# Opening, neighbourhood diagonals and feed forward of a two-block transformer kernel: transfers reordered, six feed-forward stages in one

## The reference

```python
def first_block(x, c, ctx, c_ctx, ...):
    for l in range(2):
        shift, scale, gate = split(silu(c) @ w_mod[l] + b_mod[l], 3)      # the same for c_ctx
        h = rms_norm(x, norm_gain[l]) * (1 + scale) + shift               # hc from ctx likewise
        aq, ak, av, ag, bz, bg, nq, nk, nv, ng = split(h @ w_in[l])
        ...          # global attention, pooling, neighbourhood attention
        # the latter adds bias = rpb[:, drow, dcol], a table of relative positions
        x = x + gate * (y @ w_out[l])
    return x

def second_block(x, p, ...):
    ...              # forgetting attention and a recurrent scan
    h2 = rmsnorm(x, g_ffn)
    u = causal_dwconv(h2 @ w_up, conv_w, conv_b)          # D_FF = 2816: 2 x 22 tiles of 128
    x = x + (gelu(u[..., :D_FF]) * u[..., D_FF:]) @ w_down
    x = x + sigmoid(rmsnorm(x, g_ple) @ w_ple_gate) * (p @ w_ple_up)
    return x
```

## Time and profile before

| | us |
|---|---|
| median of 3 runs | 4183.56 |
| lowest and highest run | 4174.37, 4185.14 |
| the profiled execution | 4179.65 |
| its span, first to last instruction | 4177.9 |
| PE matmuls busy | 3622.6 (87% of the span) |
| DVE, POOL, ACT busy | 1949.7, 1606.7, 1147.7 |
| mean granted TensorE clock | 0.926 of full speed |

### The profile page before, as it was taken

The page is one execution under the profiler, slowest core; times in us unless marked ns, Lnnn a source line. Parts: engine busy times, 40 slices in busy tenths (PEclk is TensorE's granted clock), DMA queues, the critical chain, the costliest instruction groups (busy, mean ns, idle before and its releaser), DMA issues. The chain is left out here.

```text
span 4177.9 us, 59647 instructions
## 1 busy us (share of the span) xinstructions
PE 3622.6 (87%) x24988; PEld 2712.7 (65%) x24988; DVE 1949.7 (47%) x1943; ACT 1147.7 (27%) x1585; POOL 1606.7 (38%) x881
## 2 busy tenths in 40 slices
PE   4999699879899798888999977858798989989878
PEld 3788333668677334676777767734477777877767
DVE  4342566552542665533577023354543642633524
ACT  2223344330213343412344112225301320100122
POOL 0332356542343465434357333313333422423233
PEclk9999799989899799998999988868898999999989
DMA  4111200044112100122212210010041111111111
GB/s 164 36 39 66 62 1 1 14 157 148 54 36 72 19 1 14 55 108 78 81 48 77 84 42 4 4 70 1 21 160 41 45 40 45 46 45 41 39 44 68
DMA packets 93715, 226.52 MB, mean 54 GB/s; under 512 B 28320, under 2 KB 37920, under 8 KB 92464
## 3 DMA queue, kind: packets, MB, share of 16 engines
q1 hardware_dynamic: 85616, 193.86, 14.0%
q10 hardware_dynamic: 7872, 29.36, 2.0%
HBM read 184.36 MB, written 38.83 MB: 53 GB/s over the span
## 5 line engine op out<-in xcount | busy, mean ns | idle before, releaser
L265 PE MATMUL acc<-h_hi,weights_hi 128*128 128x512 f32 (+1 forms) x1152 | 452.3, 393 | 85.0 <-DVE h_lo L1879 39.7
L252 POOL TENSOR_TENSOR weights_hi<-weights,ones 128x1024 fp32r<-128x1024 f32 (+3 forms) x100 | 176.4, 1764 | 775.8 <-PE acc L267 775.8
L266 PE MATMUL acc<-h_lo,weights_hi 128*128 128x512 f32 (+1 forms) x1152 | 449.3, 390 | 0.0
L267 PE MATMUL acc<-h_hi,weights_lo 128*128 128x512 f32 (+1 forms) x1152 | 448.6, 389 | 0.0
L1637 PE MATMUL acc<-h_hi,weights_hi 128*128 128x512 f32 (+1 forms) x928 | 366.1, 395 | 32.3 <-DVE h_lo L1791 26.4
L1638 PE MATMUL acc<-h_lo,weights_hi 128*128 128x512 f32 (+1 forms) x928 | 340.3, 367 | 0.0
L1639 PE MATMUL acc<-h_hi,weights_lo 128*128 128x512 f32 (+1 forms) x928 | 340.3, 367 | 0.0
L957 DVE TENSOR_REDUCE part_max<-aux 128x2 f32<-128x856 f32 (+5 forms) x234 | 237.8, 1016 | 213.9 <-PE aux L823 147.6
L265 PEld LDWEIGHTS acc<-h_hi,weights_hi 128*128 128x128 f32 x1152 | 222.1, 193 | 133.2 <-issue 63.5
L2249 PE MATMUL acc<-h_hi,weights_hi 128*128 128x512 f32 x672 | 274.3, 408 | 24.8 <-DVE h_lo L2527 14.8
L1673 POOL TENSOR_TENSOR weights_hi<-weights,ones 128x1024 fp32r<-128x1024 f32 x44 | 85.7, 1947 | 498.3 <-PE acc L1639 389.2
(11 more groups left out here) (412 smaller groups left out, 7604.1 us busy)
## 6 DMA issues: line engine op xcount, KB each, us to landing
weights<-in_w_in SPq DMA_DIRECT2D x44, 512.0 KB, 3.5
weights<-in_w_up SPq DMA_DIRECT2D x41, 512.0 KB, 3.5
arena<-in_w_mod SPq DMA_DIRECT2D x6, 2048.0 KB, 9.8
weights<-in_w_out SPq DMA_DIRECT2D x21, 512.0 KB, 4.9
weights<-in_w_mod ACTq DMA_DIRECT2D x4, 2048.0 KB, 19.5
mixer_gates<-arena SPq DMA_DIRECT2D x32, 256.0 KB, 2.0
x_between<-arena ACTq DMA_DIRECT2D x16, 512.0 KB, 3.1
weights<-in_w_gates SPq DMA_DIRECT2D x16, 512.0 KB, 3.6
```

What stands on the lines that cost most here:

```text
L265: nc.tensor.matmul(out, w.hi[:, b, k, :], hi[:, kr, cols], start=(k == 0), stop=False)
L266: nc.tensor.matmul(out, w.hi[:, b, k, :], lo[:, kr, cols], start=False, stop=False)
L267: return nc.tensor.matmul(out, w.lo[:, b, k, :], hi[:, kr, cols], start=False, stop=(k == nk - 1))
```

## The change

- Opening: SP's queue takes the small loads, x tiles 0, 2, 4, 6, then w_mod pieces 0 and 2 and the first two tiles of w_in; ACT's queue takes ctx, x tiles 1, 3, 5, 7 and w_mod pieces 1 and 3. The spreading of rstd with its three copies and POOL's parting of the first two weight tiles move from `project` into `opening` for layer 0; the buffers for them are made before it. `project` skips them there.
- Diagonals: SP issues the lower half of each head, then the two gate pieces; ACT issues the upper half of each head, one ahead of each of its four key copies.
- Feed forward: one stage, `feed_forward`, with a list of jobs of known order. Parts are 7, 7 and 8 tiles. Of a part's ups the next part's first one is done ahead of the part's eight downs, except in the last part. Every engine's program is straight code over the jobs. The first down of a part takes its last k after all others in both chunks. The conv, gelu and gating are as before; the squares at the end use the buffers of the conv.

```diff
+        def diagonals(h):
+            return bass.AP(rpb.tensor, (l * NA_HEADS + h) * 15 * RPB_ROW, [[1, GRID_W], [RPB_ROW, 15], [1, GRID_W]])
...
                 for h in range(NA_HEADS):
                     sp.wait_ge(cleared, h + 1)
-                    for a in range(2):
-                        first = (l * NA_HEADS + h) * 15 * RPB_ROW
-                        src = bass.AP(rpb.tensor, first, [[1, GRID_W], [RPB_ROW, 15], [1, GRID_W]])
-                        sp.dma_start(diag[a * 64:a * 64 + 64, h, a:a + 15, :], src).then_inc(placed[h], 16)
-                    if h < 2 and gates:
-                        gates.fetch(sp, h)
+                    sp.dma_start(diag[0:64, h, 0:15, :], diagonals(h)).then_inc(placed[h], 16)
+                for i in range(2 if gates else 0):
+                    gates.fetch(sp, i)
...
                     for half in range(2):
+                        h = 2 * i + half
+                        act.wait_ge(cleared, h + 1)
+                        act.dma_start(diag[64:P, h, 1:16, :], diagonals(h)).then_inc(placed[h], 16)
                         nc.scalar.copy(k_twice[half * HD:(half + 1) * HD, i, :], k[i * HD:(i + 1) * HD]).then_inc(rounded, 1)
...
-                sp.dma_start(x[:, :, SEQ:TOK], I["ctx"]).then_inc(x_loaded, 16)
-                for k in range(KD):
+                for k in range(0, KD, 2):
                     sp.dma_start(x[:, k, 0:SEQ], I["x"][:, k]).then_inc(tile_loaded[k], 16)
+                for i in (0, 2):
+                    m.fetch(sp, i)
+                for j in range(2):
+                    sp.dma_start(raw[:, j], I["w_in"][0, j]).then_inc(w_loaded, 16)
 
             @block.scalar
             def _(act):
-                for i in range(4):
+                act.dma_start(x[:, :, SEQ:TOK], I["ctx"]).then_inc(x_loaded, 16)
+                for k in range(1, KD, 2):
+                    act.dma_start(x[:, k, 0:SEQ], I["x"][:, k]).then_inc(tile_loaded[k], 16)
+                for i in (1, 3):
...
+                for c, (c0, cw) in enumerate(BOTH):
+                    act.wait_ge(spread, c + 1)
+                    nc.scalar.copy(rstd_all[:, c0:c0 + cw], pg.aux[:, c % 2, 0:cw]).then_inc(kept, 1)
                 for i in range(4):
                     m.keep(act, i)
+                act.wait_ge(kept, 3)
+
+            @block.gpsimd
+            def _(pool):
+                pool.wait_ge(w_loaded, 32)
+                for j in range(2):
+                    nc.gpsimd.tensor_tensor(w_hi[:, j], raw[:, j], ones, ALU.mult).then_inc(w_rounded, 1)
+                    pool.wait_ge(w_rounded, j + 1)
+                    nc.gpsimd.tensor_tensor(w_lo[:, j], raw[:, j], full(w_hi[:, j]), ALU.subtract).then_inc(w_parted, 1)
+                pool.wait_ge(w_parted, 2)
...
+                pe.wait_ge(inverted, 1)
+                for c, (c0, cw) in enumerate(BOTH):
+                    if c == 2:
+                        pe.wait_ge(kept, 1)
+                    for t in range(cw // P):
+                        mm = nc.tensor.matmul(pg.aux[:, c % 2, t * P:(t + 1) * P], pg.rstd[:, c0 // P + t:c0 // P + t + 1].to_broadcast([P, P]),
+                                              cn["ident"][:], start=True, stop=True)
+                    mm.then_inc(spread, 1)
...
-                fetch(0)
-                fetch(1)
+                if not opened:
+                    fetch(0)
+                    fetch(1)
...
+                if opened:
+                    pool.sem_inc(parted, 2)
                 for kind, i in order:
-                    if kind == "split":
+                    if kind == "split" and i >= done_before:
                         b = i % 2
-                        pool.wait_ge(loaded[b], 16 * (i // 2 + 1))
+                        pool.wait_ge(loaded[b], 16 * ((i - done_before) // 2 + 1))
...
-                    for c, (c0, cw) in enumerate(BOTH):
+                    for c, (c0, cw) in enumerate(() if opened else BOTH):
...
+                weights = pg.sbuf(feats, "weights", [P, 2, KD, P]), *pg.pair(feats, "weights", [P, 2, KD, P])
+                if l == 0:
+                    opening(pg, cn, x, spare[-1], mods[0], given, cond, weights)
                 h = pg.pair(feats, "h", [P, KD, TOK])
-                project(pg, cn, l, x, h, mix, na, pool_z, spare, mods[l], *gains, gates_dram)
+                project(pg, cn, l, x, h, mix, na, pool_z, spare, mods[l], *gains, gates_dram, weights, l == 0)
...
+def feed_forward(pg, cn, x, h, conv, conv_b, g, maker_in):
...
+    parts = [(0, 7), (7, 7), (14, 8)]
+    jobs = []
+    for p0, n in parts:
+        jobs += [("up", i, b) for i in range(p0, p0 + n) for b in range(2) if ("up", i, b) not in jobs]
+        if p0 + n < FF_TILES:
+            jobs.append(("up", p0 + n, 0))
+        jobs += [("down", p0, t) for t in range(KD)]
+    part_of = dict(parts)
+    slot = {p0 + i: i for p0, n in parts for i in range(n)}
+    downs = [job for job in jobs if job[0] == "down"]
+    ups = lambda job: 2 * job[1] + job[2]
+    tail = parts[-1][0]
+
+    def weights(j):
+        kind, i, t = jobs[j]
+        if kind == "up":
+            return weight_tiles(w_up)(i + t * FF_TILES)
+        return w_down[t:t + 1, :, i:i + part_of[i], :].rearrange("t p k n -> p (t k) n")
+
+    def depth(j):
+        return KD if jobs[j][0] == "up" else part_of[jobs[j][1]]
...
+        total, ring = raw[:, 0, 2:], [u[:, 0], u[:, 1]]
...
+                for j in range(2, len(jobs)):
+                    sp.wait_ge(w.parted, j + 1)
+                    sp.dma_start(w.raw[:, j % 2, 0:depth(j)], weights(j)).then_inc(w.loaded[j % 2], 16)
...
+                for j in range(2, len(jobs)):
+                    kind, i, t = jobs[j]
+                    pe.wait_ge(w.parted, j + 3)
+                    if jobs[j - 2][0] == "up":
+                        pe.wait_ge(raw_ready, ups(jobs[j - 2]) + 1)
+                    else:
+                        pe.wait_ge(x_added, downs.index(jobs[j - 2]) + 1)
+                    rhs, nk = h if kind == "up" else g, depth(j)
+                    if kind == "down" and t == 0:
+                        pe.wait_ge(g_parted, i + nk - 1)
+                        for c0, cols in MAIN:
+                            for k in range(nk - 1):
+                                product(j, c0, cols, k, *rhs)
+                        pe.wait_ge(g_parted, i + nk)
+                        for c0, cols in MAIN:
+                            mm = product(j, c0, cols, nk - 1, *rhs)
+                    else:
+                        for c0, cols in MAIN:
+                            for k in range(nk):
+                                mm = product(j, c0, cols, k, *rhs)
+                    mm.then_inc(acc_ready, 1)
...
+                for j in range(2, len(jobs)):
+                    b, nk = j % 2, depth(j)
+                    pool.wait_ge(w.loaded[b], 16 * (j // 2) + 16)
+                    pool.wait_ge(acc_ready, j - 1)
...
+                for j, (kind, i, t) in enumerate(jobs):
+                    if kind == "up":
+                        act.wait_ge(acc_ready, j + 1)
+                        if i >= 1:
+                            act.wait_ge(raw_used, 2 * (i - 1) + t + 1)
+                        nc.scalar.copy(raw[:, t, 2:], pg.acc[:, j % 2, 0:SEQ]).then_inc(raw_ready, 1)
...
+                    elif i == tail:
+                        act.wait_ge(x_added, downs.index((kind, i, t)) + 1)
+                        if t >= 3:
+                            act.wait_ge(sq_added, t - 2)
+                        nc.scalar.activation(ring[t % 2] if t else total, x[:, t, 0:SEQ], ACT.Square).then_inc(sq_ready, 1)
...
+                        if t == 0 and i >= 1:
+                            dve.wait_ge(g_parted, i)
...
+                        if i == tail and t == 0:
+                            dve.wait_ge(g_parted, FF_TILES)
+                        dve.wait_ge(acc_ready, j + 1)
+                        tile = x[:, t, 0:SEQ]
+                        stt(tile, pg.acc[:, j % 2, 0:SEQ], 1.0, tile, ALU.mult, ALU.add).then_inc(x_added, 1)
+                        if i == tail and t >= 2:
+                            add_squares(t - 1)
...
-        for t0 in range(0, FF_TILES, FF_PART):
-            n = min(FF_PART, FF_TILES - t0)
-            norm = lambda u, rstd_all: Norm(pg, cn, xT, h, gain("g_ffn_2"), u, rstd_all)
-            feed_forward_up(pg, h, conv, cols["conv_b_2"], t0, n, g, norm if t0 == 0 else None)
-            w_down = lambda t: I["w_down_2"][bass.ds(t, 1), :, t0:t0 + n, :].rearrange("t p k n -> p (t k) n")
-            last = t0 + n == FF_TILES
-            with ExitStack() as own:
-                squares = pg.sbuf(own, "squares", [P, 3, SEQ])
-                gemm_residual(pg, cn, w_down, KD, g, xT, [(0, SEQ, None)], n, squares=[squares[:, b] for b in range(3)] if last else None)
-            pg.end_section()
+        norm = lambda u, rstd_all: Norm(pg, cn, xT, h, gain("g_ffn_2"), u, rstd_all)
```

(67 more changed lines are left out.)

81 lines of the change are left out of this document (34 added, 47 removed).

## The result

| | before | after |
|---|---|---|
| median of 4 runs each | 4184.35 us | 4085.94 us |
| lowest and highest | 4174.37, 4186.34 | 4083.74, 4088.41 |
| profiled execution, its span | 4179.65, 4177.9 | 4087.94, 4085.9 |
| mean granted clock | 0.926 | 0.936 |

The account below looks back on a forecast made before the run. TensorE bounds the kernel wherever weights stream, so only stretches where it stands can be won. Opening -20.5, diagonals -1.9, feed forward -62.9 give -85.3 from 4179.65; with 3.9 for the median, 4098 us, range 4083 to 4124.

Parts of the forecast that it names:

- Opening, -20.5: Opening: with x and ctx first and early w_in, the first product starts at 59.1 instead of 79.6, 20.5 us less.
- the two that are left then end by 50: Opening: w_mod's last two pieces land about 43, so the remaining two of four products with additions end by 50 us.
- The opening now waits for that: Opening: POOL's parting of both w_in tiles, ending at 53.3 us, was to be what ends the block.
- Diagonals of layer 1, +4.4: Second layer's diagonals: four issues on ACT's queue delay ACT and the stage by 4.4 us, between 2.8 and 6.
- 0.95 + 4 x 0.86: Second layer's diagonals: ACT's delay as one POOL clear of 0.95 us plus four issues of 0.86, together 4.4 us.
- Diagonals of layer 0, -6.3: First layer's diagonals: leading w_mod, they let the stage end near 448.5 instead of 454.76; -6.3 us, between 0 and -8.
- Feed forward, -62.9: Feed forward: five joins go, 64.6 us, less a new wait of 1.7; -62.9 us, between -64.6 and -52.
- The matmul term: Feed forward: 3072 matmuls from job 2 on at 0.2265 us each, at the upper clock level, take 695.9 us.
- ACT held by its queue: Rival, opening: ACT's issues hold it until about 27 us, taking 6.4 us off the gain, 4105 us; chance 0.08.
- The clock sinking in a long stretch: Rival, feed forward: 544 us beyond the longest shown stretch granted 0.95, 27 us lost, 4125 us; chance 0.05.
- Straight code that starves PE: Rival, feed forward: matmuls slow without loops; gain gone at 0.2543 us each, 4201 us at 0.26; chance 0.02.
- It does not do what it says: Rival, feed forward: PE still stands where ups and downs meet, three joins at 12.9 us, 4137 us; chance 0.04.

Follow-up runs that it names:

- weights_late: Changed kernel with the first two tiles of w_in again loaded and parted in the projection, the new transfer order kept; 4094.84 us.
- old_order: Changed kernel with the opening's transfers in the order of before, w_in behind x, the rest kept; 4111.83 us.
- diag_sp: Changed kernel with all eight diagonal transfers on SP's queue, still ahead of the gate pieces, none on ACT's; 4076.77 us.
- diag_only: Kernel before with only the diagonals' part of the change; 4171.40 us, ratio to before 0.9987.
- The two repeats: Changed kernel run again unaltered, twice, beside other versions; 4092.10 and 4091.08 us, ratios to before 0.9805 and 0.9797.
- late_join: Changed kernel where SP loads the first up tile's weights behind parts one and two only after the part's last down tile is added; 4113.63 us.

## Why the prediction was right, and where it was not

- *Opening, -20.5.* -21.0, and most steps came as forecast: w_in was seen at 43.66 (44.5 expected), POOL ended at 52.76 (53.3), DVE started at 53.59 (53.9), the first product came at 58.60 (59.1). One step was wrong and stayed hidden: "the two that are left then end by 50". PE began the first of the four products only behind the spreading, at 42.03, and even without POOL the last addition ends at 52.6 (weights_late, 52.47 + 0.17); here it ended at 53.06. So "The opening now waits for that", said of POOL's parting, holds by less than half a microsecond; had POOL been done at 50, the block would still have ended near 53. That this error cost nothing is luck. The gain of 7 because POOL no longer stands beside DVE is borne out by weights_late (8.6), and old_order shows the chain behind the squares setting the end.
- *Diagonals of layer 1, +4.4.* Right in sign and mechanism (diag_sp gives it back), wrong in size: +2.4. The failed term is "0.95 + 4 x 0.86": it put all four issues between ACT's copies, but an issue runs on the sequencer beside the copy before it. Only the wait for the clear, the first issue and 0.79 us of queue stand on the path, 0.95 + 0.68 + 0.79 = 2.4.
- *Diagonals of layer 0, -6.3.* -7.9: the flips came 1.5 us after their old offset instead of 4.4, for the same reason; the second product still follows the last w_mod. The net is -5.5 instead of -1.9. In diag_only it was -5.0 by the two stages (28.4 instead of 35.3 us, 26.0 instead of 24.05).
- *Feed forward, -62.9.* -60.5. The five joins went, and the wait of 1.7 us is there, 1.57 us, at the place named. The matmul term, 3072 x 0.2265 = 695.8, came out as 698.5: in the changed kernel PE waits 3.51 us ahead of job 2 instead of 3.17, and the clock then falls for about 3.5 us (the row at 3228.03, 0.63 us; 0.69 and 0.50 granted from 3226 to 3230), where before it stayed at 1.00. This takes 1.7 us. Some 1 us stays unassigned.
- *Sum and median.* The stages say -87.0 where the sum had -85.3, by two errors of opposite sign (diagonals 3.6 better, feed forward 2.4 worse, opening 0.5 better). The profiled spans differ by 92.0 and the medians by 98.4. Of the 5.0 between stages and spans 3.4 lie between the scan's last step and the feed forward (524.6 and 521.2 us), which the change does not touch and which varies by as much between executions of one kernel. The two repeats put the medians 87.8 and 83.8 us apart (by the ratios 81.5 and 84.8). So 4086 was a series at the lower end of this kernel's runs (4079.50 to 4100.35 over all), and the rest of 98 is most likely scatter: the repeats agree with that. Why the clock is granted differently is not known.
- *The rivals.* ACT held by its queue: its seven issues took 4.2 us, squares began at 18.83; fell. The clock sinking in a long stretch: 1.00 over 704 us; fell. Straight code that starves PE: no gap by issue, 619 and 620 matmuls in 140 us late in the stage (0.226 us each), instruction transfers at 0.3% of the engines as before; fell. "It does not do what it says" fell with the waits.

## What to carry to other kernels

Between long matmul stages the cost is the standing of PE plus a few microseconds at the lower clock behind it (in the kernel before 64.6 / 5 = 12.9 us a join, in late_join 12.0): put the jobs of all stages into one list, and place a job of the other kind where the last result is awaited. In a filled DMA opening count which bytes are awaited first, not how many there are, and use the time under them for whatever needs only small data. In these runs an issue on ACT's queue cost ACT little beside a running operation, but its wait and its place ahead of the first operation do; price those, and ask who stands behind.

## What the runs showed of the hardware that I had not expected

- An issue on ACT's queue can run beside ACT's operation: in layer 1 three issues, 4.2 us together, cost ACT 0.79 us.
- Two waits of 2.44 us on a busy PE were followed, after 0.9 and 1.6 us at full speed, by some 3 us at the lower clock, and one of 3.51 us likewise after 0.8 us; waits of 1.56 and 1.57 us, and one of 3.17 us in the kernel before, were not. The length of the wait alone thus does not tell.
- DVE's additions and scalings of 8 columns stretch beside POOL's work on 1024 columns: 0.93, 1.81 and 2.21 us (L1397, L1398, at 47.56 to 50.58), against 0.17 us for the one at 50.37, behind the end of one step of POOL (50.31) and ahead of the next (50.39). Each of the three ends with a step of POOL: at 48.49, 50.33 and 52.79, where POOL's steps end at 48.46, 50.31 and 52.76.
- Unchanged stages of 255 and 900 us differ by 5 to 7 us between two executions of one kernel.
